# High and low parts of every stationary operand in alternate columns, 128 bytes off the moving operands' alignment, in a two-layer float32 decoder trunk

## What is computed

```python
for layer in range(2):
    h = rms_norm(x, mix_norm[layer])
    x = x + hybrid_mixer(h, ...)         # w_in (1024 x 3584 columns), convolution of 31 taps, pooling,
                                         # sigmoid gates, w_out (1024 x 1024)
    h = rms_norm(x, ffn_norm[layer])
    if layer % 2 == 0:
        x = x + swiglu(h, w_gate, w_up, w_down)           # dense, hidden width 2816
    else:
        for e in range(8):                                # top 2 of 8 experts, hidden width 3584
            y = y + comb[:, e:e + 1] * swiglu(t, w_gate[e], w_up[e], w_down[e])
return rms_norm(x, final_norm)
```

## Time and profile before

| | |
|---|---|
| median of 3 runs | 1426.03 us (1424.77 to 1426.03) |
| the profiled execution | 1425.24 us, of which its span is 1423.7 us |
| TensorE matmul busy | 1410.1 us (99%), 6494 matmuls |
| weight load busy | 1169.2 us (82%) |
| VectorE, ScalarE, GpSimd busy | 83%, 69%, 15% |
| granted TensorE clock | 0.997 of full |
| read from memory | 437.97 MB, 313 GB/s over the span |

### The profile page before, as it was taken

One profiled execution on the slowest core, in us unless ns is written; L12 is line 12 of the kernel. 1 busy time (PEld: TensorE's weight loads), 2 busy tenths in 40 slices (PEclk: granted clock), 3 DMA queues, 4 the chain that ended last, 5 costly groups with the idle time before them and its releaser, 6 DMA issues.

```text
span 1423.7 us, 18338 instructions
## 1 busy us (share of the span) xinstructions
PE 1410.1 (99%) x6494; PEld 1169.2 (82%) x6494; DVE 1176.6 (83%) x1067; ACT 986.4 (69%) x876; POOL 209.1 (15%) x250
## 2 busy tenths in 40 slices
PE   9999999999999999999999999999999999999997
PEld 7888888888888888888888888888888888888885
DVE  6987444548987998889899898888989989888896
ACT  7775434347765877867877777786787777778674
POOL 5840000005831101001001001000100100100010
PEclk9999999999999999999999999999999999999998
DMA  9646555545548899999999999999999999999990
GB/s 360 217 169 212 186 178 191 193 152 204 166 173 303 288 400 366 371 369 409 374 385 369 392 367 372 388 370 368 410 375 383 370 390 366 372 390 372 365 411 33
DMA packets 197551, 445.94 MB, mean 313 GB/s; under 512 B 8400, under 2 KB 19968, under 8 KB 197504
## 3 DMA queue, kind: packets, MB, share of 16 engines
q1 hardware_dynamic: 192496, 432.57, 80.2%
q0 software_dynamic: 2304, 8.39, 2.2%
q10 hardware_dynamic: 2704, 4.38, 0.9%
HBM read 437.97 MB, written 7.34 MB: 313 GB/s over the span
## 4 chain that ended last, share of the span: by engine, by line
issue 58%; PE 36%; POOL 5%; DVE 0%; ACT 0%; DMA 0%; POOLq 0%; ACTq 0%; DVEq 0%
PE bank L1470 11%; PE bank L1472 11%; PE bank L1471 11%; POOL small L616 2%; POOL gates L619 2%; POOL sums L626 1%; PE bank L1531 1%; PE bank L1634 0%; POOL work L596 0%; PE bank L1596 0%; PE bank L1776 0%; DMA work<-in_mix_norm_dram 0%; DVE w_lo L995 0%; PE bank L1590 0%; PE bank L1563 0%
## 5 line engine op out<-in xcount | busy, mean ns | idle before, releaser
L995 DVE TENSOR_TENSOR w_lo<-raw,w_hi 128x2048 fp32r<-128x2048 f32 x256 | 583.2, 2292 | 133.4 <-ACT w_hi L659 133.1
L659 ACT ACTIVATE w_hi<-raw 128x2048 fp32r<-128x2048 f32 x256 | 488.3, 1912 | 198.8 <-PE bank L1472 198.4
L1470 PE MATMUL bank<-w_hi,dT_hi 128*128 128x512 f32 (+1 forms) x756 | 296.3, 392 | 0.0
L1472 PE MATMUL bank<-w_hi,dT_lo 128*128 128x512 f32 (+1 forms) x756 | 293.1, 388 | 0.0
L1471 PE MATMUL bank<-w_lo,dT_hi 128*128 128x512 f32 (+1 forms) x756 | 292.6, 387 | 0.0
L1470 PE MATMUL bank<-w_hi,cT_hi 128*128 128x512 f32 x492 | 194.3, 395 | 0.0
L1472 PE MATMUL bank<-w_hi,cT_lo 128*128 128x512 f32 x492 | 191.7, 390 | 0.0
L1471 PE MATMUL bank<-w_lo,cT_hi 128*128 128x512 f32 x492 | 191.6, 389 | 0.0
L1472 PEld LDWEIGHTS bank<-w_hi,dT_lo 128*128 128x128 f32 x756 | 142.0, 188 | 29.3
L1470 PE MATMUL bank<-w_hi,hT_hi 128*128 128x512 f32 x416 | 164.9, 396 | 0.6 <-DVE w_lo L1092 0.6
L1470 PEld LDWEIGHTS bank<-w_hi,dT_hi 128*128 128x128 f32 x756 | 142.0, 188 | 28.3
(11 more groups left out here) (260 smaller groups left out, 1861.9 us busy)
## 6 DMA issues: line engine op xcount, KB each, us to landing
raw<-in_moe_w_gate_dram SPq DMA_DIRECT2D x96, 1024.0 KB, 7.4
raw<-in_moe_w_up_dram SPq DMA_DIRECT2D x72, 1024.0 KB, 10.3
raw<-in_moe_w_down_dram SPq DMA_DIRECT2D x72, 1024.0 KB, 8.9
raw<-in_w_in_dram SPq DMA_DIRECT2D x20, 1024.0 KB, 6.1
mix<-in_moe_w_up_dram SPq DMA_DIRECT2D x16, 1024.0 KB, 8.5
gates<-in_moe_w_down_dram SPq DMA_DIRECT2D x16, 1024.0 KB, 11.0
gates<-in_moe_w_up_dram SPq DMA_DIRECT2D x16, 1024.0 KB, 8.8
work<-in_moe_w_down_dram SPq DMA_DIRECT2D x16, 1024.0 KB, 11.1
```

The costliest lines, as they stand in the source:

```text
L659: act.activation(w_hi[split_place(u, seen.item is not None)][:, 0:width], place[slot][:, 0:width], ACT.Copy).then_inc(hi_ready, 1)
L995: dve.tensor_tensor(w_lo[split][:, 0:width], place[slot][:, 0:width], w_hi[split][:, 0:width].bitcast(F32), ALU.subtract).then_inc(lo_read ...
L1470: nc.tensor.matmul(dst, a_hi, b_hi, start=start, stop=False)
L1472: return nc.tensor.matmul(dst, a_lo, b_hi, start=False, stop=stop)
```

## The change

`hT_hi` and `hT_lo` become one buffer `hT`, and likewise `cT` and `dT`. The function `alternate` gives two views of a flat buffer, its even and its odd columns; the first is the high part, the second the low part. So the 128 values of a held operand now lie 8 bytes apart, over 1024 bytes, with the other part's values between them. All writes of held parts by ScalarE and VectorE, and VectorE's reads of them, go through the same views with the same step.

`hT` has 32 columns (128 bytes) ahead of its held part, and is that much longer. Everything that is allocated behind it lies 128 bytes further on: `cT`, `dT`, and also `tokA`, `tokP`, `tap_prod`, `gates`, `onehot`, `spreadT`, `y_hi`, `y_lo`, `row_gain`, `ident`, `mean_w`, `mix`, `taps`. `raw`, `w_hi`, `w_lo`, `xs` and `work` stay. The fourth slot of split weights is `hT[:, 0:UNIT]` and `hT[:, UNIT:2 * UNIT]`, without the 32 columns, so that it still starts at a multiple of 512 bytes and is read in neighbouring columns. `xn_lo` (used once, before the first item) is the first and second 1024 columns of `cT`, in neighbouring columns.

No instruction is added, removed or moved, on any engine, and no wait changes. Lines of the program stand 7 further down.

```diff
+HELD_AT = 32
...
-        hT_hi = sb("hT_hi", [P, KD, S], F32R)
-        hT_lo = sb("hT_lo", [P, KD, S], F32R)
+        hT = sb("hT", [P, HELD_AT + 2 * KD * S], F32R)
...
-        cT_hi = sb("cT_hi", [P, CC * S], F32R)
-        cT_lo = sb("cT_lo", [P, CC * S], F32R)
-        dT_hi = sb("dT_hi", [P, GROUPS * S], F32R)
-        dT_lo = sb("dT_lo", [P, GROUPS * S], F32R)
+        cT = sb("cT", [P, 2 * CC * S], F32R)
+        dT = sb("dT", [P, 2 * GROUPS * S], F32R)
...
+        def alternate(flat):
+
+            both = flat.rearrange("p (n two) -> p two n", two=2)
+            return both[:, 0, :], both[:, 1, :]
+
+        hT_hi, hT_lo = (part.rearrange("p (k s) -> p k s", k=KD) for part in alternate(hT[:, HELD_AT:]))
+        cT_hi, cT_lo = alternate(cT[:, :])
+        dT_hi, dT_lo = alternate(dT[:, :])
+
...
-        xn_lo = [t[:, :] for t in (cT_hi, cT_lo)]
+        xn_lo = [cT[:, b * D:(b + 1) * D] for b in range(TB)]
...
-        w_hi = [w_hi_3[:, i, :] for i in range(SPLIT)] + [hT_hi[:, :, :].rearrange("p k s -> p (k s)")]
-        w_lo = [w_lo_3[:, i, :] for i in range(SPLIT)] + [hT_lo[:, :, :].rearrange("p k s -> p (k s)")]
+        w_hi = [w_hi_3[:, i, :] for i in range(SPLIT)] + [hT[:, 0:UNIT]]
+        w_lo = [w_lo_3[:, i, :] for i in range(SPLIT)] + [hT[:, UNIT:2 * UNIT]]
```

## The result

The changed kernel takes 1449.62 us (median of 4 runs, 1449.03 to 1449.92), the kernel before 1425.4 us beside it: 1.0171 times as long, 95% interval 1.0153 to 1.0188. It is slower by 24 us, where 52 us less were forecast.

The account below looks back on a forecast made before the run. TensorE, busy 99%, was taken as the bound through its 226.7 ns between starts. Gains of 46.9, 9.3 and 5.1 us, together 61.3, less 8 for stalls, gave 53 off 1426.03: 1373 us, range 1362 to 1428.

Parts of the forecast that it names:

- the parts counted at nothing: Strided held-part writes, shifted small buffers and mixers' middles: no change taken; doubled VectorE writes, 16 us, kept for the range.
- The middle of a mixer: 26 to 84 us and its like in layer 1: VectorE busy 57.1 of 58 us, TensorE would only wait, no gain.
- 13.3 ns per matmul: Every product: time between TensorE starts beyond one column per clock at 2.4 GHz, 32 clocks, at 512 or 256 columns.
- two reads meet: Held and moving reads meet in one part of memory; an 8-byte step and 128-byte offset can remove all 32 clocks.
- the term of the held operand's new step and place: Every product in the program: 11.7 ns gain per matmul, 61.3 us together; range from nothing to all 13.3 ns.
- L1590's 215 ns: Full-float32 matmuls with new weight loads start 215 ns apart, 2 ns over their columns; 226.7 - 215.0 gave 11.7 ns gain.
- The whole 61.3 us: Gain if nobody else becomes late: items 46.9 us, dense layer 9.3, mixer ends, pooling and all-token products 5.1.
- 116 ns at L1715 for 120: 256 columns past held operands 64 bytes further on each step start 116 ns apart, taken as evidence against a fixed price.
- Each weight load starting with the matmul before it: Timeline inside an item: held values are read while moving ones are read, taken as evidence against a fixed price.
- Below nothing is possible: Held operand's step and place, every product: a loss instead of a gain, left to a rival.
- the rival of the wide operand: Every product: 1024 bytes of held values cost 64 clocks, 13.3 ns more per matmul, 76 us, 1502 us; chance 0.14.
- The first rival: Every product: the 32 clocks are no meeting of reads, held address does not matter, 226.7 ns and 1426 stay; chance 0.14.

## Why the prediction was wrong

**The reading of the bound was right.** TensorE has no slack, the distance between its starts is the time, and any distance over 226.7 ns makes the kernel slower from the first nanosecond: 2.05 us per item, 16.4 of the 24 us. Two of the parts counted at nothing were nothing: VectorE's writes did not change (685 and 686 ns), and ScalarE's 42 ns are covered. The middle of a mixer was counted at nothing for a gain; for the loss it was not: in the same 58 us TensorE starts 255 matmuls and not 262. That mixer 0's middle ends at 84.0 us in both is chance, since the changed run was four products ahead at 26 us.

**The step that failed is the one from "13.3 ns per matmul" to "two reads meet".** It put the term of the held operand's new step and place at 11.7 ns of gain per matmul; measured, it is a loss of 4.1 ns per matmul of an item, 4.8 in the settled rhythm. The prediction held three rows to be evidence against a fixed price. One was, but not for what was made of it.
- L1590's 215 ns. It was called the nearest row of a matmul that does not pay, and gave 11.7 of 13.3 ns as the gain. It is a matmul of another type, and its rows are passes, two to a matmul: 16 rows for the 8 matmuls that two mixers issue, so that a column takes two clocks per pass and four in all. In full float32 each pass starts 215.8 ns after the last at every step and offset that was tried; what a float32r matmul pays there could not be read from it. The whole 61.3 us hung on this one number.
- 116 ns at L1715 for 120. This one did say that the 13.3 ns are no fixed price at 256 columns, and the 113.3 ns above say it more strongly. It did not carry over to 512 columns: there the steady rhythm of offset 0 is the lower end of all that was measured and not the upper one. Nor to the change's own layout: its pooling products start 120.9 ns apart, where 107 to 109 were foretold.
- "Each weight load starting with the matmul before it" shows that they overlap, not that they collide. With a quarter of the held values the distance was 231.7 ns, no shorter.

**"Below nothing is possible" was underpriced.** The held operand's step and place got a range from nothing to 13.3 ns of gain, and a loss only as 13.3 ns more in the rival of the wide operand. Measured: 4.1 to 4.8 ns more. That rival had the right side and the wrong mechanism: neighbouring columns at 128 bytes, which span no more than before, lose 28 us, more than the change does. The first rival, a fixed price, was right in that no layout took the 13.3 ns of a 512-column matmul away. Its time, 1426, would have followed if address had mattered nowhere; the kernel before stands at the one place modulo 256, of those that were tried, from which the disturbed stream comes back to its shortest rhythm. The loss was there to be had, the gain at 512 columns was not.

Of the change's own arithmetic something remains: with a step of 8 bytes, offsets of 64 and 128 bytes lose less (23 and 24 us) than none (36.5). What takes 226.7 down to 213.3 was found in no layout.

The Trainium skill's statements came out unequally. "SBUF — State Buffer", section "Door 1: The DMA port swizzle", has 16-byte lines that need two hits each for the full rate. For held operands the runs agree: a load lasts 188, 193 to 197, 253 and 310 ns at steps of 4, 8, 12 and 16 bytes, hardly more at two values per line and much more at fewer. For the moving operand they do not: with two values per line, 256 columns take 230 ns instead of 120. The section "Who interferes with whom" of the same page has two independent read ports and a TensorE that waits for nobody. That other engines cost it nothing, the runs confirm (226.7 ns beside 352 GB/s of DMA and both engines). That held and moving reads are independent they do not: the distance between starts goes by where one lies from the other, and the measurement decides. The formula of "TensorE: Matmul & The Clock Gate", section "Back-to-back issue gap", from which the prediction took 10.9 ns that could go, is given there for isolated matmuls, which the prediction left out; the full-float32 passes keep it (215.8 ns), and no float32r layout of 512 columns came near it.

**What stays open.** Why float32r matmuls start 13.3 ns later than their columns take, and full-float32 passes 2.5; and what sets the patterns. The runs show that they exist, that with a step of 4 bytes the place of the held from the moving operand counts modulo 256 bytes, and that a disturbance chooses among them. Why 256 columns can have 113.3 ns and 512 never had less than 226.6 on average is open too. What in the memory or in TensorE makes the patterns was not isolated. No version was found that is faster than the kernel before.

## What to carry to other kernels

Where TensorE is the bound and its starts are evenly spaced, write the distance down and treat the place of the held operand modulo 256 bytes from the moving one as part of the design: here being off it cost 27 to 33 us of 1425 with neighbouring columns, and alternate columns cost 23 to 37 wherever they lay. A gap that is the same for every matmul is a price until a run of the same type and width of matmul shows it smaller; another type's row, however near in the code, is no evidence. And measure layouts in the company that they will have, with the transposes between, since a loose stream can sit in a rhythm that the kernel does not come back to. A small kernel of bare matmuls answers forty such questions in one run.

## What the runs showed of the hardware that was not expected

- Back-to-back float32r matmuls with 128 held columns fall into repeating patterns of starts: 227, 227, 226 ns (226.67) with 512 moving columns and both operands at the same place modulo 256 bytes, 226.7 to 234.3 otherwise with a step of 4 bytes, 230 to 236 with 8, and up to 240 with 16.
- The pattern depends on history: 16 bytes off, 226.7 ns until four transposes come between, 233.3 for the rest of the layout.
- With 256 moving columns the order can turn round: 64 bytes off, 113.3 ns in one stretch and 117.8 in another of the same run, against 120 at the same place.
- A moving float32r operand with a step of 8 bytes streams at about half the rate: 256 columns in 230 ns, against 120.
- A held operand with a step of 16 bytes has a load of 310 ns, and its matmuls still start 235 to 240 ns apart: a load longer than the distance between starts does not set that distance.
- Loading 32 held columns is recorded at 0.11 us, 128 at 0.19, and the matmuls come no sooner.
